# Slot numbers of a mixture of experts in five parts instead of four, and the last one-hot tables behind the first token block

## What is computed

```python
scores = sigmoid(t @ w_router)                       # (tokens, 16)
sel = (scores + b_router).reshape(-1, 4, 4)          # 4 groups of 4 experts
best = argmax(sum(top_k(sel, 2)))                    # one group for each token
_, local = top_k(sel[best], 2)                       # two experts of that group
w = scores[chosen] / sum(scores[chosen])
a = silu(t @ w_gate[e]) * (t @ w_up[e]) * gate[e]    # for each expert e
y = sum over e of a @ w_down[e]
```

## Time and profile before

| | |
|---|---|
| runs | 1133.07, 1135.09, 1132.86 us |
| median | 1133.07 us |
| span of the profiled execution | 1132.6 us |
| PE busy | 1065.7 us, 94% |
| DVE busy | 851.1 us, 75% |
| ACT busy | 689.5 us, 61% |
| POOL busy | 156.2 us, 14% |
| granted PE clock, mean | 0.979 |

### The profile page before, as it was taken

How to read it: one execution, slowest core, us unless ns; L and a number is a source line. 1 busy time by engine, 2 the same in 40 slices (tenths; PEclk the granted TensorE clock), 3 DMA queues, 4 the chain that set the end, 5 groups by cost and what they waited for, 6 DMA issues and landing times.

```text
span 1132.6 us, 16007 instructions
## 1 busy us (share of the span) xinstructions
PE 1065.7 (94%) x5941; PEld 839.2 (74%) x5943; DVE 851.1 (75%) x1191; ACT 689.5 (61%) x867; POOL 156.2 (14%) x184
## 2 busy tenths in 40 slices
PE   6999998897999999999989998889799999999996
PEld 3798454693888888888869975468388888888886
DVE  4345556668899888898965546765889988888896
ACT  2423555544677777777724256654467777777764
POOL 0325200330011111111040011000101111111002
PEclk7999999998999999999999999999799999999999
DMA  9997889246999999999698371004599999999951
GB/s 351 344 338 214 322 292 288 92 141 263 370 356 373 370 381 370 372 376 376 229 377 251 135 241 74 1 1 155 220 386 372 366 378 382 374 371 369 367 200 58
DMA packets 82560, 319.86 MB, mean 282 GB/s; under 512 B 22464, under 2 KB 26926, under 8 KB 69692
## 3 DMA queue, kind: packets, MB, share of 16 engines
q1 hardware_dynamic: 67232, 285.58, 68.9%
q0 software_dynamic: 14160, 30.19, 7.9%
q10 hardware_dynamic: 1100, 3.23, 0.7%
HBM read 308.05 MB, written 30.57 MB: 299 GB/s over the span
## 4 chain that ended last, share of the span: by engine, by line
PE 81%; issue 7%; DVE 5%; ACT 4%; DMA 1%; POOL 0%; SPq 0%; DVEq 0%; ACTq 0%; POOLq 0%
PE bank L1209 16%; PE bank L1201 16%; PE bank L1202 16%; PE bank L891 3%; PE bank L917 3%; PE bank L921 3%; PE bank L914 3%; PE bank L1094 3%; PE bank L1260 2%; PE bank L1108 2%; ACT work L1603 2%; PE bank L986 2%; PE bank L1126 2%; PE bank L1027 1%; PE bank L1290 1%
## 5 line engine op out<-in xcount | busy, mean ns | idle before, releaser
L1663 ACT ACTIVATE work_r<-ring 128x4096 fp32r<-128x4096 f32 x93 | 338.1, 3636 | 120.0 <-PE bank L1202 108.6
L2244 DVE TENSOR_TENSOR ring_r<-ring,work_r 128x4096 fp32r<-128x4096 f32 x92 | 404.1, 4417 | 5.6 <-ACT work_r L1663 5.6
L1201 PE MATMUL bank<-work_r 128*128 128x512 f32 x768 | 305.2, 397 | 3.4 <-issue 3.1
L1202 PE MATMUL bank<-work_r 128*128 128x512 f32 x768 | 300.1, 391 | 0.0
L1209 PE MATMUL bank<-ring_r,work_r 128*128 128x512 f32 x768 | 193.8, 394 | 0.0
L1201 PEld LDWEIGHTS bank<-work_r 128*128 128x128 f32 x768 | 144.8, 188 | 33.9 <-issue 3.9
L1209 PEld LDWEIGHTS bank<-ring_r,work_r 128*128 128x128 f32 x768 | 143.7, 188 | 32.3
L1202 PEld LDWEIGHTS bank<-work_r 128*128 128x128 f32 x768 | 144.5, 188 | 28.7
L2507 POOL DMA_INDIRECT work<-hscr,idx x32 | 38.9, 1216 | 360.8 <-PE bank L1260 248.7
L1519 ACT ACTIVATE work_r<-ring 128x512 fp32r<-128x512 f32 (+1 forms) x48 | 28.8, 603 | 71.5 <-PE bank L921 71.5
L1943 DVE TENSOR_TENSOR ring_r<-ring,work_r 128x512 fp32r<-128x512 f32 (+1 forms) x48 | 32.1, 676 | 51.7 <-ACT work_r L1519 51.6
(11 more groups left out here) (270 smaller groups left out, 1546.5 us busy)
## 6 DMA issues: line engine op xcount, KB each, us to landing
ring<-in_w_gate SPq DMA_DIRECT2D x32, 2048.0 KB, 10.8
ring<-in_w_up SPq DMA_DIRECT2D x32, 2048.0 KB, 11.7
ring<-in_w_down SPq DMA_DIRECT2D x32, 2048.0 KB, 11.4
ring<-in_w_ada SPq DMA_DIRECT2D x24, 2048.0 KB, 9.9
ring<-in_w_in SPq DMA_DIRECT2D x4, 2048.0 KB, 15.8
yscr<-hT POOLq DMA_DIRECT2D x2, 3072.0 KB, 13.2
ring<-yscr SPq DMA_DIRECT2D x6, 1024.0 KB, 7.3
ring<-in_w_out SPq DMA_DIRECT2D x4, 1280.0 KB, 7.0
```

The source lines that it names most:

```text
L1201: mm(b[:], x_hi[:, k, :], hi[:, k, half, :], start=(k == 0), stop=False)
L1202: last = mm(b[:], x_lo[:, k, :], hi[:, k, half, :], start=False, stop=False)
L1663: A_(w_hi[:, slot % 2, :], ring[slot][:], ACT.Copy).then_inc(s_hi, 1)
L2244: tt(ring_r[slot][:], ring[slot][:], w_hi[:, slot % 2, :].bitcast(F32), ALU.subtract).then_inc(s_lo, 1)
```

## The change

The experts' slot numbers are made in five parts, `PARTS_OF_SLOTS`: expert 0 alone, experts 1 to 3, and then the three other groups of four. All counts of semaphores follow. What moves:

- part 0 is `onehots(0)`, `by_slot(0)`, `slots(0)` for expert 0 only: tables of 128 x 128 instead of 128 x 512, 3 matmuls instead of 12.
- part 1 (experts 1 to 3) is new: DVE makes its tables (128 x 384) behind `slots(0)`, and calls `slots(1)` ahead of the tables of the groups that follow. PE's `by_slot(1)` (9 matmuls) stands behind `route[3]` or the ten filling matmuls, ahead of `tokens(0)`.
- the tables of the last group, `onehots(4)`, stand behind `first_expert_low(1)` and ahead of `rest(0, 1, 1)`.
- `by_slot(2)` and `by_slot(3)` stand where `by_slot(1)` and `by_slot(2)` stood, `by_slot(4)` where `by_slot(3)` stood.

```diff
+PARTS_OF_SLOTS = ((0, 1), (1, 4), (4, 8), (8, 12), (12, 16))
+NPS = len(PARTS_OF_SLOTS)
...
+def part_of(e):
...
+    return [a <= e < b for a, b in PARTS_OF_SLOTS].index(True)
...
-        bS = (bY[1], bY[0], bA, bY[1])
+        bS = (bY[1], bY[1], bY[0], bA, bY[1])
...
                         for _ in range(10):
                             mm(bG[:], onesb[:], swab[:], start=True, stop=True)
+                    by_slot(1)
...
                     def slots_in_gate():
-                        by_slot(1)
                         by_slot(2)
+                        by_slot(3)
 
                     def slots_in_up():
-                        by_slot(3)
+                        by_slot(4)
                         weights_by_slot()
...
                     onehots(0)
                     slots(0)
+                    onehots(1)
                     if p == 0:
                         for j in route[2] if l else []:
                             ada(l, j)
+                    slots(1)
                     if p:
                         rest(0, 0, 0)
-                    for q in range(1, NG):
+                    for q in range(2, NPS if p else NPS - 1):
                         onehots(q)
...
                     if p == 0:
                         first_expert_low(1).then_inc(s_lo, 1)
+                        onehots(NPS - 1)
                     rest(0, 1, 1)
...
-                    slots(1)
                     slots(2)
+                    slots(3)
                     rest(1, 0, place(0, 0)[0])
-                    slots(3)
+                    slots(4)
...
-                            g.wait_ge(s_slot, NG * n + min((e + 2) // EPG, NG - 1) + 1)
+                            g.wait_ge(s_slot, NPS * n + part_of(e + 2) + 1)
```

More of the change, by code:

```diff
@@ L1220, in by_slot @@
                     def by_slot(q):
-                        pe.wait_ge(s_oneh, n * NG + q + 1)
-                        if q == NG - 1:
-                            pe.wait_ge(s_slot, n * NG + 1)
+                        pe.wait_ge(s_oneh, n * NPS + q + 1)
+                        if q == NPS - 1:
+                            pe.wait_ge(s_slot, n * NPS + 2)
+                        first, end = PARTS_OF_SLOTS[q]
                         for t in range(NT):
-                            for e in range(EPG):
-                                last = mm(bS[q][:, 4 * e:4 * e + 4], onehot[:, q, t, e, :], vals[:, t, q * EPG + e, 0:4],
-                                          start=(t == 0 and e == 0), stop=(t == NT - 1), skip_group_check=True)
+                            for e in range(first, end):
+                                last = mm(bS[q][:, 4 * (e - first):4 * (e - first) + 4], onehot[:, e // EPG, t, e % EPG, :],
+                                          vals[:, t, e, 0:4], start=(t == 0 and e == first), stop=(t == NT - 1), skip_group_check=True)
                         last.then_inc(s_slotp, 1)
@@ L2219, in slots @@
                     def slots(q):
[L2221 to L2225, removed]
+                        first, end = PARTS_OF_SLOTS[q]
+                        v.wait_ge(s_slotp, NPS * n + q + 1)
+                        pairs = bS[q][:, 0:4 * (end - first)].rearrange("p (e c b) -> p e c b", e=end - first, c=2)
+                        sums = slotf[:, first // EPG, first % EPG:first % EPG + end - first]
+                        nc.vector.tensor_reduce(sums, pairs, AX.X, ALU.add).then_inc(s_slotf, 1)
+                        v.wait_ge(s_slotf, NPS * n + q + 1)
+                        ts(idx[:, first:end, :], sums, BIG, None, ALU.add).then_inc(s_slot, 1)
                     def gate_weights():
@@ L2233, in onehots @@
                     def onehots(q):
+                        first, end = PARTS_OF_SLOTS[q]
                         for t in range(NT):
-                            ins = tt(onehot[:, q, t], iotab[:].unsqueeze(1).to_broadcast([P, EPG, P]),
-                                     rk[:, t, q * EPG:(q + 1) * EPG].unsqueeze(2).to_broadcast([P, EPG, P]), ALU.is_equal)
+                            ins = tt(onehot[:, first // EPG, t, first % EPG:first % EPG + end - first],
+                                     iotab[:].unsqueeze(1).to_broadcast([P, end - first, P]),
+                                     rk[:, t, first:end].unsqueeze(2).to_broadcast([P, end - first, P]), ALU.is_equal)
                         ins.then_inc(s_oneh, 1)
@@ L2553, in count_passes_left @@
                     g.wait_ge(s_as, NE * done)
[L2554 removed]
+                    for s, k in ((s_slotp, NPS), (s_slotw, 1), (s_xt, NE), (s_hu, MOE_CH), (s_gd, NE), (s_gu, NE), (s_at, NE), (s_y, NE),
                                  (s_xhigh, 1), (s_xh, NE), (s_hi, MOE_CH), (s_sg, NE), (s_ah, NE), (s_ys, NE),
[L2556 removed]
+                                 (s_rest, 2), (s_oneh, NPS), (s_slotf, NPS), (s_slot, NPS), (s_gsl, 1), (s_gcol, NE), (s_xlow, 1),
                                  (s_xs, NE), (s_lo, MOE_CH), (s_a, NE), (s_as, NE), (s_further, 1)):
```

2 lines of the change are left out of this document (removed).

## The result

| | before | after |
|---|---|---|
| first comparison, median | 1133.03 us (4 runs, 1132.86 to 1135.09) | 1142.78 us (4 runs, 1142.56 to 1144.37) |
| ratio, 95% interval | | 1.0083 [1.0069, 1.0096] |
| second comparison, median | 1134.66 us (25 runs, 1132.11 to 1138.12) | 1140.70 us (6 runs, 1139.11 to 1144.35) |
| ratio, 95% interval | | 1.0048 [1.0031, 1.0065] |
| span of the profiled execution | 1132.6 us | 1140.9 us |

What follows compares the result with a forecast made beforehand. PE bounds the kernel with no later idle time among the experts, so delays at the two starts carry through: 3.5 us in layer 0 plus 4.0 in layer 1 on 1133.07 us gives 1140.6 us, range 1136.9 to 1142.8.

Steps and rivals of the forecast that it cites:

- one term of 1.7 us: Layer 1's start: a fall to half clock after 2.6 us of PE idle time, costing 1.6 to 1.75 us.
- expert 1's gather: Layer 1: issued at 820.0, landing at 825.5 or 830.6, wanted at 829.9 or 831.6; 0 to 0.7 us, taken as nothing.
- The step that decides: Both starts: DVE waits for PE's part 1 ahead of six tables; layer 1's product 2.3 us late, layer 0's 1.8 or 3.1.
- Layer 0: Start of the experts: six fills end last, 3.1 us late at half clock, plus some 0.4 us behind; 3.5 us.
- an earlier rise of the clock: Layer 0, before the last modulation transposes: 0.25 us (0 to 0.5) taken off PE's time.
- The clock in layer 1: Layer 1's start: a drop to half clock held likelier than not, 1.7 us, making the layer's loss 4.0 us.
- rival (a): Clock stays full in layer 1, falls in layer 0 only: 5.8 us, 1138.9 us; chance 0.19.
- the row at 567.7: Profile of the kernel before: PE idle 2.40 us with the clock staying full, cited for the lesser case.
- The long bound of the forecast: Expert 1's gather in layer 1: landing 10.6 us after issue beside weight loads, at 830.6.
- The moved tables: Last three tables behind the gate block's second half: DVE 1.83 us later against PE, covered, no cost.
- margin that the working left to `weights`: Tightest hand-over behind the moved tables: 0.2 us left of 2.04; if gone, a few tenths a layer.
- The sum: Whole kernel: 3.5 us in layer 0 plus 4.0 in layer 1, 7.5 us slower, 1140.6 us; chance 0.60.

Runs made afterwards that it cites:

- PE early: Changed kernel with PE's nine matmuls of part 1 right behind `by_slot(0)`, ahead of the modulation jobs and ten fills; 1135.29 us, ratio 1.0013.
- fill in the gap: Changed kernel with 15 filling matmuls behind expert 0's token transposes in layer 0, where PE was idle; 1142.30 us, ratio 1.0067.
- after, loads wait: Changed kernel with SP holding back the weight loads until expert 1's gather has landed too; 1141.52 us, ratio 1.006.
- last tables only: Kernel before with only the last group's tables moved behind `first_expert_low(1)`; 1134.28 us, ratio 0.9995.
- after again: Changed kernel once more, word for word, for a second trace; 1140.70 us, ratio 1.0048.
- loads wait: The version tables first, with SP also holding the weight loads until expert 1's gather has landed; 1135.48 us, ratio 1.0005.
- mended both ways: The version loads wait, plus in layer 1 `by_slot(1)` right behind `by_slot(0)` and `slots(1)` right behind the modulation pieces; 1135.07 us, ratio 1.0006.
- tables first: Changed kernel with DVE's `slots(1)` moved behind the six tables, modulation pieces and count; PE untouched; 1141.45 us, ratio 1.0068.
- both mended: Changed kernel with `slots(1)` behind the six tables and count, and part 0 made experts 0 and 1; 1134.93 us, ratio 1.0004.
- two experts: Changed kernel with part 0 made experts 0 and 1, part 1 experts 2 and 3; DVE's wait stays; 1144.14 us, ratio 1.0094.
- delay of 14: Kernel before with 20 instead of 6 filling matmuls in layer 0; 1137.32 us, ratio 1.0028.
- before again: Kernel before once more, word for word, for a second trace; 1134.44 us, ratio 1.001.

## Why the prediction was right, and where it was not

The median, 1142.78 us, lies 2.2 us above the forecast and just inside its upper end. The second comparison, 1140.70 us, lies on it as a time, but the kernel before was slower beside it: the differences are 9.75 and 6.0 us, and 7.5 were forecast. The direction and the mechanism, DVE's wait in front of six tables, were right. That the total is near is in part luck: one term of 1.7 us did not come, and two others took its place, expert 1's gather, which the sum had at nothing, and the middle, which it did not have.

**The step that decides was right.** DVE was to wait about 4.7 us in front of six tables: 4.56 us in layer 1 and 3.74 in layer 0, in the second trace 4.56 and 4.41. Expert 0's gather left at 277.01 in layer 0, where 277.1 was forecast. The product of layer 1 was to be 2.3 us late and is 2.29 us late. PE early shows that it is the place of the answer, not the work: the same instructions, with nine matmuls moved, cost nothing that can be measured.

**Layer 0 was near.** Forecast 3.5 us, measured 3.1 and 3.9. The first product came 2.58 us late, where 3.1 were forecast at half clock: `by_slot(1)` was done at 281.24 and not 281.7, the six tables at 285.25 and not 285.7. The working took off 0.25 us for an earlier rise of the clock; it rose 3.4 us earlier here. In the second trace it stayed at half until 280.3, and `by_slot(1)` was done 0.66 us later against the rank matmul. Another 0.5 us was lost behind the first product, in the second trace 1.5, where 0.4 (0 to 1.0) had been taken. The fall of the clock behind 3.67 us of idle time came as forecast, and fill in the gap prices it at 1.1 to 1.2 us or a little more.

**The clock in layer 1 was wrong.** A fall was forecast, at 1.7 us. The idle stretch was 2.40 us long and the clock stayed full, in both traces of after; that is rival (a) in this point. Behind idle stretches of 2.80 us at that place it fell in fill in the gap and in after, loads wait. A gap of the length of the row at 567.7 was set against one of 2.18 us behind which the clock had fallen, and nothing in the rows told which would hold. Taken as a rule for every gap, the advice of the Trainium skill (TensorE: Matmul & The Clock Gate, "Why this matters for your kernels") gave a drop here that did not come; the page gives it for longer gaps than this one.

**Expert 1's gather was mis-sized.** The term was taken at nothing, with 0.7 us as its bound, and measured 1.0 us in layer 1 (3.25 of the piece less 2.29 of the first product), in the second trace 0.6. The working was good up to its last step. Put on the time scale of before (layer 1 begins 5.29 us later here), the gather left at 819.43 us and landed 11.5 us later at 830.9:

```profile
DMA to landing us min/median/max: 11.5/11.5/11.5
```

The long bound of the forecast had given 830.6, and PE wanted the tokens at 829.9, to the tenth as forecast. So the value to take was the long one, as the prediction itself said of the row with 10.6 us; it took nothing, and by its own working that held only if the clock's loss delayed PE (tokens wanted at 831.6); that loss did not come. Two terms of one sum excluded each other there.

**The moved tables** cost nothing, as forecast; last tables only shows it alone. The 0.2 us of margin that the working left to `weights` were measured there as 0.22.

**The sum.** Forecast 3.5 + 4.0 = 7.5. The two pieces gave 3.09 + 3.25 = 6.3 us in the first trace and 3.88 + 2.93 = 6.8 in the second. All ten runs of after have a median of 1141.9 us, some 7.4 us above the medians of before in the later groups. What is left beside the pieces, in the profiled executions, is the middle: 2.3 and 3.6 us against the first trace of before, 1.7 and 3.0 against the second, with 6.8 us of half clock in the attention of layer 1. The prediction had no term for it. In the medians, 7.4 us less the two pieces leave only about 1 us for it.

**What stays open.** Whether that stretch belongs to the change. It stands at 686 to 700 us in the traces of after, after again, PE early, loads wait and mended both ways, and not in tables first, fill in the gap, both mended and after, loads wait, which split the slot work in a similar way; two experts and delay of 14 have 3.4 us of half clock from about 727 us instead. It is absent from all three traces with the parts of before and no delay (before, before again, last tables only). The two kernels with the shortest L0, 1.9 us below before, had it and gained nothing. One trace of a kernel can't tell whether it always has it. Other falls in the middle differ between traces of one kernel too: before has half clock from 589.4 to 592.8 and from 794.2 to 801.1 us, before again from 568.2 to 571.6 and from 793.5 to 796.9. The traces also differ by up to 4.6 us in a place that no edit reaches: the rank matmul of layer 0 comes between 269.13 (before again) and 273.78 us. Part of the spread of 1131 to 1141 us between runs of one kernel thus lies ahead of anything that was changed. Why the two comparisons give 9.75 and 6.0 us was not shown; the first has four runs of each kernel.

The Trainium skill (TensorE: Matmul & The Clock Gate, "What's actually happening") says that the chip judges PE's activity on a schedule that runs on by itself and isn't reset when a kernel starts. The traces agree in so far as one kernel's half clock moves between its executions: 691.8 to 698.6 us and 693.3 to 700.1 us in the two of after. That it accounts for the stretch in the middle was not shown.

## What to carry to other kernels

Before a step is split so that its first part is ready sooner, look at where the second part's answer stands on the other engine: a wait is as long as the queue ahead of the instruction that ends it, here modulation jobs and ten fills ahead of nine small matmuls. Look then for the wait behind the wait; with one of two of nearly equal size removed the time did not move, and only both together gave it back. And where one term of a sum is nothing only because another one comes, work out both cases to the end: if the other doesn't come, the first has its full price.

## What the runs showed of the chip that was not expected

- **A gather beside weight loads.** The same kind of indirect DMA landed 3.4 to 5.5 us after its issue where the weight loads were held back or were issued only after it. Expert 1's landed after 10.9 to 11.5 us where they ran beside it (after, after again, tables first), and those of experts 2 and 3 in the same traces after 5.0 to 15.8 us. In layer 0 of after it is 3.7 us for expert 0's and 11.2 us for expert 1's, issued 4.9 us later. Holding the loads back gave 4.2 us (loads wait). The experts behind it took no longer for that: from the end of L0 to the last product with lower weights in layer 0 it is 279.1 us with the hold and without it (loads wait, tables first).
- **The clock behind idle stretches of nearly one length.** Full behind 2.40 us at 567.7, behind 2.40 us in layer 1 of after, and behind 3.17 us at 570.6 in after, loads wait; half behind 2.18 us at 101.3, behind 2.80 us in layer 1 of two experiments, and behind 3.67 us in layer 0. The stretch at 567.7 stands in before again at 563.5, 3.35 us long, and there the clock fell to half from 568.2 to 571.6 us. Length alone didn't sort them.
- **Half clock in the midst of busy matmuls.** At 694 to 699.5 us in after again PE was busy 5.45 of 5.5 us and ran at 0.50; in PE early it was busy 6.00 of 6.00 us from 691 to 697, at 0.50. In all five traces with the stretch the clock falls at nearly the same point of the program, between two idle stretches of PE of 1.04 and 1.15 us or up to 0.8 us behind the second. The same two stand in before again (they end at 684.53 and 686.57 us), where the clock stayed full, so they alone don't bring it on. What does was not found out.
